# Summing the expert rows on TensorE by four picks instead of by two

## What is computed

```
gate = softmax(best, axis=-1)
u = expert_u[experts]
vsel = expert_v[experts]
act = gelu(einsum('thkd,td->thk', u, hb))
return einsum('thk,thkd->td', gate * act, vsel)
```

## Time and profile before

| | us |
|---|---|
| runs, median of 3 | 1970.48 |
| runs, lowest and highest | 1958.55, 1972.49 |
| the profiled execution's own time | 1974.7 |
| its span in the profile | 1972.9 |
| PE busy | 1670.4 (85%) |
| DVE busy | 748.8 (38%) |
| ACT busy | 464.2 (24%) |
| POOL busy | 291.1 (15%) |
| granted TensorE clock, mean | 0.911 |

### The profile page before, as it was taken

The page is one execution under the profiler, slowest core; times in us unless marked ns, Lnnn a source line. Parts: engine busy times, 40 slices in busy tenths (PEclk is TensorE's granted clock), DMA queues, the critical chain, the costliest instruction groups (busy, mean ns, idle before and its releaser), DMA issues.

```text
span 1972.9 us, 16022 instructions
## 1 busy us (share of the span) xinstructions
PE 1670.4 (85%) x5752; PEld 853.5 (43%) x5752; DVE 748.8 (38%) x1829; ACT 464.2 (24%) x1240; POOL 291.1 (15%) x268
## 2 busy tenths in 40 slices
PE   6998976767669996887669977898999969999998
PEld 3444454324234531323223322344444446678853
DVE  3643164645695566566653342121000141200001
ACT  3311131422332223234333421121111021210000
POOL 0000001322433233234332222000000000000000
PEclk8999987788879997998789998899998969999999
DMA  9524306799999999999999999575983403244441
GB/s 356 211 86 171 149 20 247 281 413 379 412 388 392 404 414 414 409 408 411 413 403 371 381 410 384 177 265 186 300 283 124 152 19 122 92 128 147 152 154 59
DMA packets 185055, 527.10 MB, mean 267 GB/s; under 512 B 6880, under 2 KB 74464, under 8 KB 151568
## 3 DMA queue, kind: packets, MB, share of 16 engines
q1 hardware_dynamic: 146672, 251.13, 36.0%
q0 software_dynamic: 37584, 270.75, 33.8%
q10 hardware_dynamic: 720, 4.19, 0.6%
HBM read 525.00 MB, written 1.05 MB: 267 GB/s over the span
## 4 chain that ended last, share of the span: by engine, by line
PE 67%; DMA 19%; DVE 7%; ACT 4%; issue 2%; POOL 1%; SPq 0%; POOLq 0%; DVEq 0%; ACTq 0%
PE bank L1032 13%; PE bank L629 9%; DMA arena<-in_peer_rows,pidx 9%; PE bank L741 7%; PE bank L1149 6%; DMA ring<-in_ffn_w_gu 5%; PE bank L690 4%; PE bank L661 4%; PE bank L1109 3%; PE bank L816 3%; PE bank L672 2%; DMA ring<-in_peer_w_query 2%; PE bank L996 2%; PE bank L1005 2%; DVE arena L2364 2%
## 5 line engine op out<-in xcount | busy, mean ns | idle before, releaser
L1842 POOL DMA_INDIRECT arena<-in_peer_rows,pidx x256 | 286.3, 1118 | 904.7 <-PE bank L1149 581.4
L1149 PE MATMUL bank<-arena,keep 128*32 128x512 f32 x1024 | 283.1, 704 | 128.3 <-ACT keep L1715 128.0
L2364 DVE SCALAR_TENSOR_TENSOR arena<-arena,ring 128x1024 f32<-128x1024 f32 x256 | 305.6, 1223 | 164.9 <-DMA arena<-in_peer_rows,pidx 163.9
L1032 PE MATMUL bank<-ring,hT_all 128*128 128x512 f32 x608 | 283.2, 624 | 31.6 <-DMA ring<-in_ffn_w_gu 17.2
L1032 PEld LDWEIGHTS bank<-ring,hT_all 128*128 128x128 f32 x608 | 119.4, 200 | 188.7 <-issue 164.3
L1149 PEld LDWEIGHTS bank<-arena,keep 128*32 128x32 f32 x1024 | 53.4, 121 | 311.4 <-ACT keep L1715 182.9
L629 PE MATMUL bank<-hT_all,ring 128*128 128x256 f32 x832 | 185.3, 386 | 1.3 <-ACT hT_all L1354 1.3
L629 PEld LDWEIGHTS bank<-hT_all,ring 128*128 128x128 f32 x832 | 161.5, 194 | 24.8 <-ACT hT_all L1354 1.0
L1702 ACT ACTIVATE pf<-pf 128x2 f32<-128x2 f32 x128 | 25.8, 202 | 354.2 <-DVE arena L2364 353.9
L816 PE MATMUL bank<-hT_all,ring 128*128 128x128 f32 (+1 forms) x384 | 67.6, 342 | 28.2 <-DMA ring<-in_peer_w_query 25.0
L741 PE MATMUL bank<-ring,hT_all 128*128 128x512 f32 x192 | 88.5, 619 | 3.0 <-DVE hT_all L1979 3.0
(11 more groups left out here) (374 smaller groups left out, 1731.3 us busy)
## 6 DMA issues: line engine op xcount, KB each, us to landing
ring<-in_ffn_w_gu SPq DMA_DIRECT2D x66, 1024.0 KB
ring<-in_ffn_w_down SPq DMA_DIRECT2D x13, 2048.0 KB
ring<-in_w_mod SPq DMA_DIRECT2D x12, 2048.0 KB
ring<-in_conv_w_in SPq DMA_DIRECT2D x12, 2048.0 KB
ring<-in_mem_w_kv SPq DMA_DIRECT2D x8, 2048.0 KB
ring<-in_w_in SPq DMA_DIRECT2D x6, 2048.0 KB
ring<-in_mem_w_q SPq DMA_DIRECT2D x6, 2048.0 KB
ring<-in_mem_w_o SPq DMA_DIRECT2D x6, 2048.0 KB
```

The costliest lines, as they stand in the source:

```text
L1032: m = mm(b[:, :], src[:, k], slot8[w][:, k], start=(k == 0), stop=(k == KC - 1))
L1149: m = mm(acc[b][r:r + 32, :], diag[n % 8], vslot[n % SLOTS][:, b * 512:(b + 1) * 512], start=(n % 128 < 4), stop=(n % 128 >= 124))
L1842: nc.gpsimd.indirect_dma_start(out=row_in[n % SLOTS], out_offset=None, in_=a["peer_rows"], in_offset=bass.IndirectOffsetOnAxis(ap=pidx[:, ...
L2364: stt(uslot[n % SLOTS], uslot[n % SLOTS], 1.0, h2g[n % 4], ALU.mult, ALU.mult, accum_out=pact2[:, 16 * (g % 2) + k:16 * (g % 2) + k + 1]). ...
```

## The change

For n0 % 4 == 0 PE still does the works tied to n0, but leaves the pair for later. For n0 % 4 == 2 it does its works, waits until the diagonals of picks up to n0 + 1 are there, and then sums the four picks n0 - 2 to n0 + 1: all four into the first half, then all four into the second. So the pairs' waits for `diag_ready` are 64 instead of 128, and four increments of `v_used` come together. The number of matrix products, the bytes that are moved, and the programs of POOL, DVE, ACT and SP stay as they are.

```diff
--- before.py
+++ after.py
@@ -1141,10 +1141,12 @@
                     pe.wait_ge(sem("mem_scaled"), 2)
                 for work in PICK_WORK.get(n0, ()):
                     picks_work(work)
+                if n0 % 4 == 0:
+                    continue
                 acc = M if n0 < 128 else T
                 pe.wait_ge(sem("diag_ready"), n0 + 2)
                 for b in range(2):
-                    for n in (n0, n0 + 1):
+                    for n in range(n0 - 2, n0 + 2):
                         r = 32 * (n % 4)
                         m = mm(acc[b][r:r + 32, :], diag[n % 8], vslot[n % SLOTS][:, b * 512:(b + 1) * 512],
                                start=(n % 128 < 4), stop=(n % 128 >= 124))
```

## The result

| | runs | median us | lowest, highest | ratio to before |
|---|---|---|---|---|
| before | 11 | 1970.48 | 1958.55, 1979.41 | |
| after | 11 | 1982.90 | 1978.99, 1993.21 | 1.0076 [1.0052, 1.0099] |

The changed kernel is slower, by 12.4 us between the medians and by 0.5 to 1.0% in the interval of the ratio. Forecast was 8 us faster. The time lies in the stated range (1938 to 1993) and within 1% of before, but it moved the other way. The profiled execution has a span of 1986.0 us, 13.1 more than before, and all of it is in the picks: their last matrix product ends at 1258 us instead of 1244.

A forecast was written before the change was run, and what follows sets the result against it. The prediction saw a ring of PE, POOL, DMA engines, DVE and ACT, none bounding alone, with the mean DMA rate setting a floor. Gains of 18 us less 10 us cost gave -8 from 1970.5, some 1963 us, range 1938 to 1993.

The forecast's parts named there:

- The floor: Picks, 350 to 1244 us: 351 MB at 413 GB/s takes 849 us, so reordering PE gains at most 45 us.
- What the change removes from PE: PE's sums of the picks: runs of 16 records take 1.9 us, saving 1.9 a quad; about 140 us stay busy.
- rival C: Four tiles in one group don't stream at once, a group takes 3.8 us: 1977 us; chance 0.04.
- What it frees: Work of pair 4k+2 runs before pair 4k and its diagonals; four places on the chain together gain 18 us.
- (b): 456 to 474 us: PE's idling before pair 32 and DVE's 10.08 us wait for regrouped gates go; 4 us kept.
- (c): 592 to 675 us, PE alternating work and pairs without pause: seven groups lose 1.9 each, 13 us; 6.5 taken.
- (a): 385 to 404 us: two even pairs on the chain between query projections, ahead of a weight transfer; gain 3.8 us.
- (d): 1050 to 1244 us, PE waiting for weights and units: two or so even pairs ahead of a release; gain 4 us.
- What it adds: Even pair's slots come free later, so gathers queue later: 0.9 us for each of 11 chain pieces, 10 us cost.
- A: The ring starves, slots in fours emptying the gather queue: 3 us a chain piece, half the gains kept, 1995 us; chance 0.20.
- turning point: The starved-ring rival decides when added emptiness passes 1.6 us a chain piece, 18 against the 18 us gained.
- B: PE was the bound; its 142 us count until DMA stops them, two thirds of the 45 us: 1940 us; chance 0.28.

The follow-up runs named there:

- e3: Kernel before, with groups of four only for picks 28 to 39, pairs elsewhere; 1969.0 us, ratio 0.9991.
- e4: Kernel before, with groups of four only from pick 64 on, pairs before that; 1985.2 us, ratio 1.0084.
- e6: Kernel before, with groups of four (joint wait and release) for picks 0 to 155 only; 1972.8 us, ratio 1.0025.
- e1: Kernel before, PE order unchanged, but the even pair's slots released only with the odd pair's, by fours; 1993.6 us, ratio 1.0124.
- e2: Kernel before, even pair moved behind the odd pair's works, but summed two by two with own waits and releases; 1970.8 us, ratio 1.0007.
- e7: Kernel before in its old order, with six ring slots for gathered rows instead of eight; 2010.4 us, ratio 1.0192.
- e8: Kernel before, pairs in old order, gathering only the u half of each row (result differs); 1850.8 us, ratio 0.9392.
- e9: Changed kernel, groups of four, gathering only the u half of each row (result differs); 1822.9 us, ratio 0.9251 to the kernel before.
- e5: Kernel before, even pair moved behind the odd pair's works for picks 0 to 155 only, two by two with own waits; 1965.4 us, ratio 0.9980.

## Why the prediction failed

**The floor** was not put to the test. With full rows all kernels move the same bytes, and none got below before by more than can be measured. 351 MB at 413 GB/s are 851 us and not 849, so the most that could be won was 43 us rather than 45; nothing came near it.

**What the change removes from PE.** Right for the unit: a group takes 1.92 us at the higher clock (granted 1.00 at 598.81), and work and group alternate as expected (before, in the earlier trace rows, two pairs stood between two such works):

```profile
591.70 7.17 PE L996 MATMUL bank<-mem_all,ring 128*128 128x256 f32 x32
...
598.81 1.92 PE L1151 MATMUL bank<-arena,keep 128*32 128x512 f32 x16
...
612.65 3.64 PE L1151 MATMUL bank<-arena,keep 128*32 128x512 f32 x16 [4.59 <-ACT keep L1717]
```

So rival C is out. From the 2.38 times for three column tiles of the Trainium skill, "TensorE: Matmul & The Clock Gate", Part 3, the prediction estimated 2.4 us for a group of four. This case's traces do not agree: four tiles took 1.92 to 1.94 us where two took 1.91. The sum over the run was put at 140 us and is 174.7, 2.73 a group. The groups start after longer idling, and more of them at the lower clock (the 3.64 us rows above; PEclk 0.83 for 0.88 in the stretch). I had not priced the clock.

**What it frees.** 18 us were put down. The run that has only the late release stands 10.7 us above the changed kernel, so together the works ahead and the four tiles are worth about 11. Of the four places, (b) happened in its first part. PE and then POOL, from 450 us on:

```profile
449.83 5.99 PE L816 MATMUL bank<-hT_all,ring 128*128 128x256 f32 x27
...
461.43 3.64 PE L1151 MATMUL bank<-arena,keep 128*32 128x512 f32 x16 [5.39 <-ACT keep L1717]
...
453.29 1.08 POOL L1844 DMA_INDIRECT arena<-in_peer_rows,pidx  x1 [0.30 <-issue]
465.83 1.52 POOL L1844 DMA_INDIRECT arena<-in_peer_rows,pidx  x1 [11.46 <-PE bank L1151]
```

```profile
459.98 0.29 DVE L2300 TENSOR_TENSOR s_all<-bank,keep 128x128 f32<-128x128 f32 x1
```

The works ran before the group at 461.43, and DVE had the regrouped gates at 459.98 instead of 471.50, without a wait. I had written that PE's idling before pair 32 would go too; 5.39 us of the 6.60 are left. And in the same rows POOL stands 11.46 us until 465.83, since the slots of picks 32 and 33 came free with 34 and 35, and e3 shows that fours at this place alone gain nothing that can be measured. (c) went the other way: group 612.65 waited 4.59 us for diagonals, at a place where PE had gone without a pause. For (a) and (d) no run was made that has them alone; in e4 and e6 no gain is seen.

**What it adds** is the step that failed: the 10 us for slots that come free later, 0.9 for each of 11 gather pieces on the chain, in a range of 0 to 55. e1 measured the late release by itself, in the old order of PE: 23.8 us. Three things were wrong. I took the dense stretches, where a pair waits for PE with its rows landed, as the nearest rows, and nine of the 11 gather pieces lay in windows where PE is busy 82.3 us of 100 or less. I priced the hold as the time between two places in PE's program and gave no price of its own to the joint wait for two pairs' diagonals, where both pairs follow their rows as they land: e2 without it is 12.1 us faster, about half of the 23.8. And I took an emptied queue to cost a fifth of the rate, from a stretch with weights under way (329 for 420 GB/s); at 530 to 536 us there are none under way, and 190 are left of 418.

The sum was -18 + 10; the runs make it about -11 + 24 = +13, for 12.4 measured. That is no check of the two terms, since the 11 is e1 less the changed kernel: only their sum and the 24 were measured. That the time lies in the stated range is owed to its width, which held both signs; the forecast's own balance, gains above the cost, was wrong.

**Rivals.** A, to which I gave 0.20, was the mechanism, by e1 and e7. Its signs in the profile were half there: DVE's waits rose to 239 us (I had set 250), the stretch fell to 389 GB/s (I had set 380), and the loss is half of its 24. Its turning point, 1.6 us a piece, has been passed: 24 / 11 = 2.2. B had its condition wrong: e8 and e9 are the case in which PE's work counts, and there the groups of four win. Its 1940 us were not tested.

## What to carry to other kernels

A ring of slots has a lead, and a consumer that frees its slots in larger groups shortens it, even when it does less work. Before grouping, ask what the first member of a group waits for once the last one is late; price that wait by the gap between their arrivals, in the stretch where arrivals set the pace and not where the consumer is behind. If the engine already overlaps neighbours that are both ready, as PE did here with two waits in its queue, keep the waits apart.

When two streams share the DMA engines, look at the bytes of both up to a fixed time and not only at the landings of one: one can be early at the other's cost. Neither foretells the end: e2 had moved 3.6 MB more than before by 860 us and was no faster.

## What was unexpected in the hardware

Two groups of matrix products on different column tiles overlap in full though each has its own semaphore wait ahead of it, if both waits are already met: 16 records in 1.94 us at 881.38 in e2, where 8 take 1.91. The row at 719.48 of the kernel before was of this kind too, so the prediction could have seen that the joint wait is not needed for it. Where the second pair's diagonals come only as the first one ends, as for pair 80 behind pair 78 at 600.80, the two take 3.84 us.

Open: why moving the pairs helps rows come some 14 us earlier at pick 159 in e2 without any of it being left at the end. The bytes of e5 say that part of it was borrowed from the weights; how much the held pair at 872.90 cost beside that was not measured by itself.
